# Three Strassen blocks per feed-forward instead of two, with two of the four weight sums made by adding DMAs from GpSimd's queue

## The reference

```
D_MODEL, SEQ, DEPTH, D_FF = 1024, 256, 2, 2816
def _swiglu(h, w_gate, w_up, w_down):
    return (silu(h @ w_gate) * (h @ w_up)) @ w_down
for l in range(DEPTH):
    x = x + 0.5 * _swiglu(_rms_norm(x, ffn1_norm[l]), ffn1_w_gate[l], ffn1_w_up[l], ffn1_w_down[l])
    x = x + mixer(_rms_norm(x, mix_norm[l]))          # rotary angles: positions * inv_freq, cos, sin
    x = x + 0.5 * _swiglu(_rms_norm(x, ffn2_norm[l]), ffn2_w_gate[l], ffn2_w_up[l], ffn2_w_down[l])
```

## Time and profile before

| | |
|---|---|
| median of 3 runs | 1025.47 us (1024.95 to 1027.05) |
| profiled execution | 1025.66 us, its span 1023.9 us |
| PE busy | 1018.2 us (99%), 4905 matmuls |
| DVE busy | 846.4 us (83%) |
| ACT busy | 660.8 us (65%) |
| GpSimd busy | 330.8 us (32%) |
| DMA | 208.99 MB, mean 204 GB/s |
| feed-forwards | about 0 to 185, 340 to 517, 517 to 692, 845 to 1024 us |

### The profile page before, as it was taken

One profiled execution on the slowest core, in us unless ns is written; L12 is line 12 of the kernel. 1 busy time (PEld: TensorE's weight loads), 2 busy tenths in 40 slices (PEclk: granted clock), 3 DMA queues, 4 the chain that ended last, 5 costly groups with the idle time before them and its releaser, 6 DMA issues.

```text
span 1023.9 us, 13331 instructions
## 1 busy us (share of the span) xinstructions
PE 1018.2 (99%) x4905; PEld 853.9 (83%) x4905; DVE 846.4 (83%) x1008; ACT 660.8 (65%) x836; POOL 330.8 (32%) x258
## 2 busy tenths in 40 slices
PE   9999999999999999999999999999999999999998
PEld 6888888998888888888888888889988888888887
DVE  6999977698976898888679889866999678988972
ACT  6767665576874575766557666647778556666761
POOL 2999400138850100000049990001589300000000
PEclk9999999999999999999999999999999999999999
DMA  8968578555544596748749574975366365947491
GB/s 278 309 191 277 162 209 274 160 185 176 207 161 128 182 328 183 244 140 234 228 154 339 166 226 135 274 248 174 127 214 226 123 173 185 331 140 233 158 240 42
DMA packets 175185, 208.99 MB, mean 204 GB/s; under 512 B 64112, under 2 KB 129936, under 8 KB 175120
## 3 DMA queue, kind: packets, MB, share of 16 engines
q1 hardware_dynamic: 173904, 206.03, 64.9%
q10 hardware_dynamic: 1216, 2.11, 0.7%
HBM read 192.90 MB, written 1.05 MB: 189 GB/s over the span
## 4 chain that ended last, share of the span: by engine, by line
PE 98%; ACT 1%; DVE 1%; DMA 0%; issue 0%; POOL 0%; ACTq 0%
PE bank L829 30%; PE bank L831 30%; PE bank L830 30%; PE bank L966 1%; PE bank L1128 1%; PE bank L1137 1%; PE bank L1158 1%; PE bank L868 0%; PE bank L1136 0%; PE bank L1160 0%; PE bank L836 0%; DMA cacc<-in_ffn_norm 0%; DVE htok L1902 0%; DVE x L1950 0%; ACT htok L1357 0%; PE bank L1146 0%
## 5 line engine op out<-in xcount | busy, mean ns | idle before, releaser
L1854 DVE TENSOR_TENSOR wlo<-raw,whi 128x2048 fp32r<-128x2048 f32 (+2 forms) x136 | 308.9, 2283 | 21.0 <-ACT whi L1344 21.0
L1344 ACT ACTIVATE whi<-raw 128x2048 fp32r<-128x2048 f32 (+2 forms) x160 | 302.9, 1910 | 25.3 <-DMA raw<-in_ffn_w_down 16.5
L829 PE MATMUL bank<-whi,hThi 128*128 128x512 f32 (+1 forms) x816 | 316.1, 387 | 0.0
L831 PE MATMUL bank<-whi,hTlo 128*128 128x512 f32 (+1 forms) x816 | 311.4, 382 | 0.0
L830 PE MATMUL bank<-wlo,hThi 128*128 128x512 f32 (+1 forms) x816 | 311.3, 381 | 0.0
L697 POOL TENSOR_TENSOR small<-small,expo 128x1 f32<-128x1 f32 (+3 forms) x20 | 30.0, 1505 | 470.5 <-DVE small L1895 432.9
L831 PEld LDWEIGHTS bank<-whi,hTlo 128*128 128x128 f32 x816 | 153.2, 188 | 29.6
L829 PEld LDWEIGHTS bank<-whi,hThi 128*128 128x128 f32 x816 | 153.3, 188 | 28.8
L830 PEld LDWEIGHTS bank<-wlo,hThi 128*128 128x128 f32 x816 | 153.4, 188 | 28.4
L829 PE MATMUL bank<-whi,gThi 128*128 128x512 f32 (+1 forms) x416 | 162.3, 390 | 0.0
L831 PE MATMUL bank<-whi,gTlo 128*128 128x512 f32 (+1 forms) x416 | 161.2, 388 | 0.0
(11 more groups left out here) (201 smaller groups left out, 1359.0 us busy)
## 6 DMA issues: line engine op xcount, KB each, us to landing
raw<-in_ffn_w_down SPq DMA_DIRECT2D x88, 512.0 KB, 4.7
raw<-in_ffn_w_gate SPq DMA_DIRECT2D x68, 512.0 KB, 4.2
raw<-in_ffn_w_up SPq DMA_DIRECT2D x68, 512.0 KB, 5.2
raw<-in_w_in SPq DMA_DIRECT2D x48, 512.0 KB, 4.9
htok<-in_ffn_w_gate SPq DMA_DIRECT2D x16, 512.0 KB, 6.1
heads<-in_ffn_w_up SPq DMA_DIRECT2D x16, 512.0 KB, 6.8
raw<-in_w_out SPq DMA_DIRECT2D x16, 512.0 KB, 4.6
raw<-in_w_in SPq DMA_DIRECT2D x8, 544.0 KB, 5.2
```

What stands on the lines that cost most here:

```text
L829: nc.tensor.matmul(out, lh, rh, start=start, stop=False, skip_group_check=skip)
L831: return nc.tensor.matmul(out, ll, rh, start=False, stop=stop, skip_group_check=skip)
L1344: nc.scalar.activation(whi[:, slot(u, RING), 0:USED[u]], src, ACT.Copy).then_inc(whi_ready, 1)
L1854: nc.vector.tensor_tensor(wlo[:, slot(u, RING), 0:n], src, whi[:, slot(u, RING), 0:n].bitcast(F32), ALU.subtract).then_inc(wlo_ready, 1)
```

## The change

1. `BLK` becomes (2, 5, 8): three blocks, chunks (2, 3), (5, 6) and (8, 9), and plain chunks 0, 1, 4, 7, 10.
2. T3 and T4 are no longer added by DVE. GpSimd's queue issues one accumulating DMA for each, from the raw slot in SBUF onto the chain buffer (1 MB read and added). SP's waits for the slots follow the DMA's count of 16.
3. These DMAs are put into GpSimd's list: block 2's before the rotary angles, block 5's after 20 of the 36 angle steps, block 8's after the rest; in the second feed-forward all behind the norm's roots.
4. The joins of chunks 0 to 7 move from DVE to ACT (`act_join`).
5. The lists of SP, PE, ACT and DVE are rewritten for it.

```diff
-BLK = (4, 7)
+BLK = (2, 5, 8)
-SUM = {"T1": 1, "T2": 1, "T3": 1, "T4": 1}
+SUM = {"T1": 1, "T2": 1, "T3": 16, "T4": 16}
...
-                if name == "B22":
+                if name == "B21":
+                    sp.wait_ge(sum_ready["T4"], per_block(l, f, c) * SUM["T4"])
+                elif name == "B22":
                     sp.wait_ge(sum_ready["T2"], per_block(l, f, c))
-                    sp.wait_ge(sum_ready["T3"], per_block(l, f, c))
-                elif name == "B21":
-                    sp.wait_ge(sum_ready["T4"], per_block(l, f, c))
+                    sp.wait_ge(sum_ready["T3"], per_block(l, f, c) * SUM["T3"])
...
-                gate_up(l, f, 2, 0)
-                gate_up(l, f, 2, 1)
                 down(l, f, 0)
+                chain_load(l, f, 2, 0)
+                chain_load(l, f, 2, 1)
+                lower_load(l, f, 2, "B22")
+                lower_load(l, f, 2, "B21")
                 turn(0)
-                gate_up(l, f, 3, 0)
-                gate_up(l, f, 3, 1)
                 down(l, f, 1)
+                gate_up(l, f, 4, 0)
                 turn(1)
-                chain_load(l, f, 4, 0)
-                chain_load(l, f, 4, 1)
+                gate_up(l, f, 4, 1)
+                chain_load(l, f, 5, 0)
                 down(l, f, 2)
...
+            def add_rows(l, f, c, name, lower):
+
+                done = per_block(l, f, c)
+                u = unit_block(f, c, lower)
+                pool.wait_ge(raw_landed[raw_slot(l, u)], raw_count(l, u))
+                if name == "T3":
+                    pool.wait_ge(chain_landed[1], done * 32)
+                    pool.wait_ge(sum_ready["T1"], done)
+                    dst = chain[1]
+                if name == "T4":
+                    pool.wait_ge(wlo_ready, l * U_LAYER + unit_block(f, c, "T2") + 1)
+                    dst = chain[0]
+                nc.gpsimd.dma_start(dst, raw[:, raw_slot(l, u), 0:2048], accum_op=ALU.add).then_inc(sum_ready[name], 16)
+
+            def first_sums(l, f):
+
+                add_rows(l, f, 2, "T3", "B22")
+                add_rows(l, f, 2, "T4", "B21")
...
             for l in range(DEPTH):
                 norm(l, 0)
+                first_sums(l, 0)
...
                 turns(K2, two_pi)
                 for part in parts:
                     less(K2, part)
+                second_sums(l, 0)
                 less(KH, parts_big[3])
...
                 assert rstep[0] == N_ROPE
+                third_sums(l, 0)
                 norm(l, 1)
...
                 norm(l, 2)
+                first_sums(l, 1)
+                second_sums(l, 1)
+                third_sums(l, 1)
...
                 first()
-                pair(2)
-                pair(3)
-                strassen(4)
-                pair(6)
-                strassen(7)
-                pair(9)
+                strassen(2)
+                pair(4)
+                strassen(5)
+                pair(7)
+                strassen(8)
                 last()
...
+                def act_join(c):
+
+                    act.wait_ge(turned_landed, per_turn(l, f, c) * 16)
+                    if c:
+                        act.wait_ge(glo, per_ffn(l, f, c - 1, 1))
+                    nc.scalar.activation(g_turned.bitcast(U16).rearrange("p (n b) -> p b n", b=2),
+                                         turned.rearrange("p (b j) r -> p b (j r)", b=2), ACT.Copy).then_inc(joined, 1)
```

More of the change, by code:

```diff
@@ L1535, in ffn @@
                 split_planes(0, 1)
-                gate_split(2, 1)
+                first_of(2, "B11")
+                down_split(0)
                 silu(1, 0)
-                down_split(0)
+                act_join(0)
+                round_joined(0)
+                sum_of(2, "T1")
                 silu(1, 1)
-                round_joined(0)
                 mixed_round()
+                sum_of(2, "T2")
+                keep(2, 0, "B11")
+                lower(2, "B22")
+                lower(2, "B21")
@@ L1573, in ffn @@
-                gate_split(6, 1)
+                sum_of(5, "T2")
+                lower(5, "B22")
+                keep(5, 0, "B11")
+                lower(5, "B21")
+                keep(5, 1, "T1")
                 split_planes(4, 0)
-                block_silu(4, 1)
+                sum_of(5, "T3")
                 split_planes(4, 1)
+                sum_of(5, "T4")
+                keep(5, 2, "T2")
                 down_split(4)
-                first_of(7, "B11")
+                act_join(4)
@@ L1601, in ffn @@
-                block_silu(7, 0)
-                gate_split(9, 1)
-                block_silu(7, 1)
-                split_planes(7, 0)
+                silu(7, 0)
+                sum_of(8, "T1")
+                split_planes(7, 0)
+                act_join(6)
+                round_joined(6)
+                sum_of(8, "T2")
+                silu(7, 1)
+                keep(8, 0, "B11")
+                lower(8, "B22")
+                lower(8, "B21")
                 split_planes(7, 1)
+                sum_of(8, "T3")
@@ L2108, in ffn @@
-                join(0)
+                of_chain(2, "B11")
+                add_T1(2)
                 down_split(0)
+                rest_joined(0)
+                of_chain(2, "T1")
+                add_T2(2)
+                mixed_rest()
+                of_chain(2, "T2")
                 mul(1, 0)
                 mul(1, 1)
-                rest_joined(0)
-                mixed_rest()
-                gate_split(3, 0)
-                mul(2, 0)
-                join(1)
-                gate_split(3, 1)
+                lower(2, "B22")
@@ L2118, in ffn @@
+                lower(2, "B21")
+                of_chain(2, "T3")
+                up_first(2)
+                of_chain(2, "T4")
                 down_split(1)
-                of_chain(4, "B11")
-                mul(2, 1)
                 rest_joined(1)
-                add_T1(4)
+                gate_first(2)
+                up_second(2)
+                gate_second(2)
+                gate_split(4, 0)
+                block_mul(2, 0)
+                block_mul(2, 1)
+                gate_split(4, 1)
@@ L2123, in ffn @@
                 down_split(2)
-                of_chain(4, "T1")
-                join(2)
-                add_T2(4)
+                mul(4, 0)
+                of_chain(5, "B11")
                 rest_joined(2)
-                mul(3, 0)
-                add_T3(4)
-                of_chain(4, "T2")
-                mul(3, 1)
-                lower(4, "B22")
-                add_T4(4)
-                lower(4, "B21")
-                of_chain(4, "T3")
-                join(3)
-                of_chain(4, "T4")
@@ L2148, in ffn @@
+                lower(5, "B21")
+                of_chain(5, "T3")
+                of_chain(5, "T4")
+                up_first(5)
                 down_split(4)
-                join(4)
-                of_chain(7, "B11")
-                add_T1(7)
                 rest_joined(4)
+                gate_first(5)
+                up_second(5)
+                gate_second(5)
+                block_mul(5, 0)
+                block_mul(5, 1)
+                gate_split(7, 0)
+                gate_split(7, 1)
@@ L2153, in ffn @@
                 down_split(5)
-                mul(6, 0)
-                mul(6, 1)
-                join(5)
-                of_chain(7, "T1")
+                of_chain(8, "B11")
                 rest_joined(5)
-                add_T2(7)
-                add_T3(7)
-                of_chain(7, "T2")
-                lower(7, "B22")
-                add_T4(7)
-                lower(7, "B21")
-                of_chain(7, "T3")
-                join(6)
-                of_chain(7, "T4")
-                gate_first(7)
+                add_T1(8)
```

190 lines of the change are left out of this document (91 added, 99 removed).

## The result

The changed kernel takes 1056.53 us (median of 4 runs, 1054.75 to 1062.28) beside 1025.34 of the kernel before on the same chip: ratio 1.031, 95% interval 1.0278 to 1.0343. It is slower by 31 us; 1044 had been forecast. The profiled execution took 1054.97 us, its span is 1053.0.

The account below looks back on a forecast made before the run. PE was taken as the bound, busy 1018 of 1023.9 us, with DVE second. Fewer matmuls -10.9, chunk 2 +16.7 and angles +13 gave +18.8, 1044.5, median 1044; forecast's own range 1030 to 1062, overall 1016 to 1064.

Parts of the forecast that it names:

- The chain at chunk 2: Opening of each feed-forward: late mixed input delays PE, 3.6 us in three and 5.9 in the first, +16.7 (7.9 to 17).
- T4 of block 2: Its adding DMA was taken as 7 us (3.4 to 12); up to 7.1 costs nothing, each microsecond above costs four.
- Rival B: Slow adding DMA delays T4 of block 2 and T3 of block 5: 12 us gives 1074, 9 gives 1056; 0.15 for above 1062.
- The angles: GpSimd's angles delay T3 of block 5: 6.5 us in each layer's first feed-forward, together +13 (0 to 40).
- rival A: GpSimd not held: DVE's gaps let the angles' part one fit in 43 us; 1022.5, or 1014.6 if all is hidden; chance 0.25.
- S + 80: S is the start of a feed-forward's gate_up(0,0); GpSimd at T3 of block 5 before S + 80 would mean case A.
- The rest of a feed-forward: Block 8 directly before chunk 10: 0 to 1 us each, taken as 0; other moves lie under PE.
- rival C: The clock falls in PE's stalls: six stalls each bringing half of 5.44 us, +16, 1060; chance 0.05.
- -10.9: PE, four feed-forwards: one more block in each saves 12 matmuls at 0.227 us, called a certain gain.

Follow-up runs that it names:

- The order of the turn alone: Changed kernel with turn(0) ahead of the load of B21 of block 2 in SP's list: 1050.49 us, ratio 1.0245.
- mixed input: Changed kernel with the mixed input left out and the plain input read in its place (output not the reference's): 1055.86 us, ratio 1.0322.
- keep: Changed kernel with the keep of T2's result moved ahead of T4's rounding in ACT's list, blocks 5 and 8: 1057.35 us, ratio 1.0316.
- The angles' cut: Changed kernel with the rotary angles cut after 12 of 36 steps instead of 20: 1058.17 us, ratio 1.0317.
- the held clock: Changed kernel with matmuls on zeros ahead of five long PE waits and T4's bank wait moved ahead of T3: 1059.67 us, ratio 1.0331.

## Why the prediction was right, and where it was not

The time lies in the forecast's own range of 1030 to 1062, 12 us above the forecast 1044. The direction and the place were right by their mechanism. That the sum came near is in part luck, as the terms below show.

**Direction and place: right, and shown.** The block at chunk 2, with the order that it brings, starves PE. The kernel with blocks at 2 and 8 has it and is as slow as the changed one; the one with 5 and 8 has not, and 22.6 of the 28.6 us are gone. The order of the turn alone is worth 6.

**The chain at chunk 2: right step by step.** In the second feed-forward all stands 11.6 us later than in the kernel before, because the first is that much longer. Shifted by this, `mixed_rest` was forecast to end at 385.6 and ended at 384.4, T2's remainder at 387.9 (386.6), T1 was forecast at 385.6 and began at 384.49. In the very first one D0 was forecast at 39.0 and began at 38.38, T1 at 47.0 (46.20). D0 of the later ones was forecast late by 1.0 and was late by 0.2 to 0.4. The term was +16.7. The later starts of D0 and T1 together are 11.5 in four feed-forwards (4.0, 2.5, 2.5, 2.5), inside the bounds of 7.9 to 17. The refilling and the lower clock behind three of them, which the term did not hold, bring them to 16.9; that this is the forecast number is luck.

**What the term left out: the rest of the opening.** The openings lost 25.9, not 16.7. T4 of block 2 was allowed a DMA of 7.1 and forecast at no cost. The DMA takes 8.3 to 8.6 at the median, once 10.4, and T4 started late by 1.6, 0.4, 3.1 and 0.3 us, 5.4 in all, 7.3 with what follows. This is the step that was mis-sized by most: the two sums that I costed at 0 are worth 22 us in the three-block kernel. A DMA slower than DVE is not the reason (with DVE adding it is 1059.75); T3 and T4 come at the end of a chain that has no lead. In the kernel before, whose first block stands after four plain chunks, the same DMAs in its second feed-forwards cost 0. The Trainium skill (DMA: Bandwidth & Descriptors, Anatomy of one DMA) gives for a plain copy of this size, as an estimate by its formula, 4.4 us; the accumulation took nearly twice that, 8.3 at the median, and no run here shows the plain copy.

**Rival B's number came, not its account.** It gave 1056 for a DMA of 9 us, and the result is 1056.53 with 8.3 to 8.6. B put 8 us on T4 of block 2 and 4 on T3 of block 5, on top of +13 for the angles. The kernel in which DVE adds, without any such DMA, is as slow, so the DMA's length alone is not what makes 1056.

**The angles: +13 forecast, at most 4 found.** The step that failed is the length of the part, and in it the premise that DVE's density in that stretch would not be lower than before. It fell from 96% and 91% to 82% and 77%, and the part from 66 and 61 us to 42.6 and 38: rival A's 43 us. GpSimd came to T3 of block 5 at S + 75 in layer 1, earlier than the S + 80 that I had named as the sign of being wrong. The contention itself is as forecast. (The Trainium skill, SBUF — State Buffer, Who interferes with whom: a DVE instruction with two SBUF inputs contends with a GpSimd instruction that reads SBUF. The trace after agrees: operations of 0.19 stand beside ones of 1.9 to 2.3 us, and each of the long ones lies under such a DVE instruction.) The first 16 `ang` operations took 10.2 and 6.3 us, 20 in layer 0 of the kernel before. What is left of the hold is small and by another path than forecast: T3's DMA goes out 3 us before T4's, T4's takes 10.4 instead of 8.4, and a keep waits behind it on ACT. That is the stall of 2.44 us before T3 of block 5 in layer 0, 4.1 with the lower clock, and 0.3 in layer 1. With the turn earlier the hold came in one of two layers at 7.13 us; 6.5 had been forecast, but through T3's own remainder, which was only 2.5 late.

**The rest of a feed-forward.** I took 0. D7 waits 0.8 in each (about 1.0 with refilling, the top of the 0 to 1 that I gave): 4 us. With DVE adding the two sums it is the same 4 us, with the sums left out it is gone. The keep that frees T2's bank stands behind T4's rounding in ACT's list and so behind T4's DMA. I had not looked at what stands behind an ACT instruction that waits for a DMA. The join on ACT takes 1.37 us instead of 1.06; alone it costs nothing.

**The clock (rival C): seen.** It fell at five stalls, 8 us in all by PE's timeline. With it held, the time was no shorter.

**The errors offset in part:** +16.7 was 25.9, +13 did not come as such, and the rest of the feed-forwards, taken as 0, was 14.6 (with the 4 at T3 of block 5). Sum -10.9 + 40 = +29 against +18.8.

**Why no single repair helped.** A wait on PE also gives DVE, ACT and the loads time. Take it away and PE reaches the next link that much sooner. Two kernels showed it directly (mixed input, keep): the wait aimed at is gone, others have grown, the time is the same. The angles' cut moved a wait to block 8 in the same way; the held clock and DVE's sums fit it. What helped is a shorter chain at its head (the turn, 6 us) or at its end (the sums, 22), or more plain work ahead of the block (22.6).

**Open.** The kernel with blocks at 5 and 8 is still 6 us above the one before; its profiled execution is 8.5 above. There D7 explains 4.2, T3 of block 8 1.9, and PE reaches the first gate product 1.4 later; the rest was not traced to a row. Why T4 and D7 are late by just these amounts was not separated into DMA, turns of g (5.0 against 3.6 us with and without the sums) and ACT's order: with DVE adding, the turns take 4.0, and the kernel is no faster. A kernel with three blocks and more plain chunks ahead of the first was not built: with 11 chunks and a plain last one, blocks would stand back to back and share `kept` and two banks.

## What to carry to other kernels

Cost a rearrangement by how far ahead of TensorE the side engines are at that place, not by their load over the whole: here a denser stage right after a start, before a lead exists, lost its gain and more, and repairing one link mostly moved the wait to the next. To find which part of a change does it, move the part as a whole (two blocks at two places) before taking away single waits. And when one engine waits for a transfer, read on in its list: what stands behind it may be what TensorE needs. When a run brings no gain, look whether the wait it was aimed at went away or moved; the time alone doesn't tell.

## What the runs showed of the hardware

- An accumulating DMA of 1 MB from SBUF onto SBUF took 8.2 to 9.4 us at the median of its groups, where a load of 512 KB took 7.1. Issued 3 us behind another such DMA it took 10.4 and 10.7 us, and 0.65 us behind one 12.9.
- The issue of a transpose in SP's queue takes longer while such a DMA runs. SP's timeline of the changed kernel:

```profile
392.08 3.78 SPq L537 DMA_TRANSPOSE qkT<-qkT  x1
```

  In the kernel before the one of that chunk took 1.23 us (at 379.98). Nine issues of 3.4 to 4.7 us stand in the changed kernel's trace, each while a DMA of T4 is under way; with DVE adding, those of the same places take 1.2 to 1.8. One of 3.4 us (at 25.8) stands before the first such DMA, in both kernels, so it is not their only cause. The load behind this one in the queue starts only when it is over, at 395.96.
- ACT's copy that puts 16-bit planes together takes 1.37 us where DVE's takes 0.755, and ACT's copy that takes them apart 1.06.
- With matmuls on zeros ahead of five stalls the granted clock was 1.000 in two of four executions, and the time was no shorter (1056.7 and 1057.3 us).
